# An expert mixer walked in pairs: the large and the small item by turns in parts, instead of one after the other

## The reference

```python
probs = jax.nn.softmax((xt @ router).astype(jnp.float32), axis=-1)
top_p, top_i = lax.top_k(probs, TOP_K)                 # TOP_K = 2 of 8
gates = ...                                            # normalised top_p, 0 elsewhere
for e in range(N_EXPERTS):
    y = y + gates[:, e:e + 1] * swiglu(xt, w_gate_up[e], w_down[e])
```

## Time and profile before

| | us |
|---|---|
| three runs | 1141.86 median, 1139.15 to 1142.47 |
| the profiled execution | 1141.93 |
| its span, first to last instruction | 1140.2 |
| PE busy | 1088.6 (95%) |
| PEld busy | 808.9 (71%) |
| DVE busy | 626.2 (55%) |
| ACT busy | 522.5 (46%) |
| first large unit of the mixer on PE | at 437.89 |
| first large unit of pairs 1, 2, 3 | at 611.00, 783.89, 958.09 |
| last small unit ends on PE | at 1126.66 |

### The profile page before, as it was taken

How to read it: one execution, slowest core, us unless ns; L and a number is a source line. 1 busy time by engine, 2 the same in 40 slices (tenths; PEclk the granted TensorE clock), 3 DMA queues, 4 the chain that set the end, 5 groups by cost and what they waited for, 6 DMA issues and landing times.

```text
span 1140.2 us, 15874 instructions
## 1 busy us (share of the span) xinstructions
PE 1088.6 (95%) x5832; PEld 808.9 (71%) x5832; DVE 626.2 (55%) x710; ACT 522.5 (46%) x576; POOL 23.2 (2%) x94
## 2 busy tenths in 40 slices
PE   9998999999999999999998999998999998999994
PEld 8876888888898787787355787354787445787451
DVE  6865555455654458895106895106897105897102
ACT  6555444344445644775015775014775004676001
POOL 2100000000000000000000000000000000000000
PEclk9999999999999999999999999999999999999998
DMA  9933556555454423998999999999999999999994
GB/s 347 356 112 111 181 182 192 185 185 188 162 176 149 138 77 117 367 362 298 343 417 408 402 418 409 359 416 409 403 418 408 333 413 411 405 414 409 358 412 204
DMA packets 110935, 343.47 MB, mean 301 GB/s; under 512 B 11613, under 2 KB 38282, under 8 KB 100618
## 3 DMA queue, kind: packets, MB, share of 16 engines
q1 hardware_dynamic: 110714, 341.93, 79.6%
q10 hardware_dynamic: 144, 0.52, 0.1%
HBM read 341.37 MB, written 1.05 MB: 300 GB/s over the span
## 4 chain that ended last, share of the span: by engine, by line
PE 78%; DVE 8%; DMA 7%; ACT 3%; issue 2%; SPq 1%; POOL 0%; POOLq 0%; ACTq 0%; DVEq 0%
PE ps L1483 22%; PE ps L1478 18%; PE ps L1480 18%; PE ps L1479 18%; DMA raw<-moe_w_gate_up_dram 5%; DMA raw<-moe_w_down_dram 2%; ACT whi L561 2%; DVE wlo L960 1%; SPq L369 1%; PE ps L1823 1%; DVE wlo L947 1%; DVE wlo L949 1%; DVE h L1212 1%; ACT xs L561 1%; PE ps L1867 1%
## 5 line engine op out<-in xcount | busy, mean ns | idle before, releaser
L561 ACT ACTIVATE whi<-raw 128x2048 fp32r<-128x2048 f32 (+2 forms) x203 | 341.7, 1688 | 247.8 <-PE ps L1480 226.5
L960 DVE TENSOR_TENSOR wlo<-raw,whi 128x2048 fp32r<-128x2048 f32 x151 | 345.4, 2292 | 121.7 <-ACT whi L561 120.6
L1478 PE MATMUL ps<-whi,xhi 128*128 128x512 f32 (+3 forms) x688 | 264.1, 384 | 18.6 <-DVE wlo L960 12.0
L1480 PE MATMUL ps<-wlo,xhi 128*128 128x512 f32 (+3 forms) x688 | 259.4, 377 | 0.0
L1479 PE MATMUL ps<-whi,xlo 128*128 128x512 f32 (+3 forms) x688 | 259.1, 377 | 0.0
L1478 PEld LDWEIGHTS ps<-whi,xhi 128*128 128x128 f32 x688 | 129.5, 188 | 48.3 <-issue 9.2
L1483 PE MATMUL ps<-raw,xs 128*64 128x512 f32 (+2 forms) x1024 | 155.0, 460 | 0.0
L1480 PEld LDWEIGHTS ps<-wlo,xhi 128*128 128x128 f32 x688 | 129.3, 188 | 23.9
L1479 PEld LDWEIGHTS ps<-whi,xlo 128*128 128x128 f32 x688 | 129.5, 188 | 22.1
L1483 PEld LDWEIGHTS ps<-raw,xs 128*64 128x64 f32 x1024 | 68.2, 137 | 81.7 <-issue 71.5
L1478 PE MATMUL ps<-whi,hhi 128*128 128x512 f32 x264 | 105.9, 401 | 0.0
(11 more groups left out here) (298 smaller groups left out, 976.8 us busy)
## 6 DMA issues: line engine op xcount, KB each, us to landing
raw<-moe_w_gate_up_dram SPq DMA_DIRECT2D x256, 512.0 KB, 12.6
raw<-moe_w_down_dram SPq DMA_DIRECT2D x80, 1024.0 KB, 17.0
raw<-moe_w_gate_up_dram SPq DMA_DIRECT2D x96, 384.0 KB, 9.4
raw<-ffn_w_gate_up_dram SPq DMA_DIRECT2D x44, 512.0 KB, 4.9
raw<-ffn_w_down_dram SPq DMA_DIRECT2D x22, 512.0 KB, 4.3
raw<-kv_shared_w_dram SPq DMA_DIRECT2D x16, 512.0 KB, 4.2
raw<-moe_w_gate_up_dram SPq DMA_DIRECT2D x32, 256.0 KB, 9.7
raw<-moe_w_down_dram SPq DMA_DIRECT2D x16, 512.0 KB, 17.9
```

The source lines that it names most:

```text
L561: return nc.scalar.activation(o, i, ACT.Copy, scale=scale)
L960: V.tensor_tensor(wlo[:, s, :].rearrange("p a w -> p (a w)"), raw[:, (hh // 2) % RAW, :], whi[:, s, :].bitcast(F32).rearrange("p a w -> p ...
L1478: pe.matmul(o, a_hi, b_hi, start=start, stop=False, skip_group_check=True)
L1480: return pe.matmul(o, a_hi, b_lo, start=False, stop=stop, skip_group_check=True)
```

## The change

Large and small item of a pair are now worked on by turns: large units 0 to 7, small 0 to 7, large 8 to 15, small 8 to 15, large 16 to 21, small 16 to 21, large 22 to 32, small 22 to 32. Transfers are issued in that order. The large item's groups are transposed after small units 1, 4, 9, 12, 17, 19; the small item's after large units 10, 18, 23, 25. Both gathers for the next pair stand after large unit 27; the large scatter stands after small unit 29, the small scatter after unit 0 of the next pair. Both selections of a pair are transposed in that pair (after large unit 5), ACT copies them out, and POOL's part in `selT` goes away. The rotary products use all 128 rows: `krT` has two copies with the other half zero. Some tensors share memory in another way, and the all-minus-one matrices are made later. What a unit, a gather or a scatter computes stays the same.

```diff
+PARTS = ((0, 8), (8, 16), (16, 22), (22, 33))
+PAIR = [(small, x) for first, end in PARTS for small in (False, True) for x in range(first, end)]
+PLACE = {unit: n for n, unit in enumerate(PAIR)}
...
+            def slot_free(n, p, previous):
+
+                if previous is None and n < RAW:
+                    sp_eng.wait_ge(lo_made, 2 * (U_MOE + n - RAW) + 2)
+                    return
+                small, x = PAIR[n - RAW]
+                of = previous if n < RAW else p
+                if small:
+                    sp_eng.wait_ge(small_used, of * FU + x + 1)
+                else:
+                    sp_eng.wait_ge(lo_made, of * FH + H_MOE + 2 * x + 2)
...
+            pair_loads(0, None, w, None, range(PARTS[0][1]))
+            sp_eng.wait_ge(items_ready, 3)
+            pair_loads(0, None, w, at(1), range(PARTS[0][1], len(PAIR)))
```

On ACT:

```diff
+            def pair(p, split, first=False, last=False):
+
+                for x in range(split, 8):
+                    item_high(x, p)
+                if first:
+                    gathered_small(p)
+                act.wait_ge(sel_tr, p + 1)
+                copy(selT[:, :], ps[:, TR_BANK, 0:SEQ]).then_inc(selT_ready, 1)
+                copy(selTs[:, :], ps[:, TR_BANK, SEQ:2 * SEQ]).then_inc(selT_ready, 1)
+                for part in range(3):
+                    silu(2 * part, p)
+                    silu(2 * part + 1, p)
+                    high(2 * part, p)
+                    high(2 * part + 1, p)
+                    x = 8 * part + (8 if part < 2 else 6)
+                    for n in range(3):
+                        item_high(x + n, p)
+                    small_silu_of(part, p)
+                    item_high(x + 3, p)
+                    hidden(part, p)
+                    if part == 2:
+                        small_silu_of(3, p)
+                    item_high(x + 4, p)
+                    if part == 2:
+                        hidden(3, p)
+                    for n in range(5, 8 if part == 0 else 6):
+                        item_high(x + n, p)
+                if not last:
+                    gathered_high(p + 1)
+                    gathered_small(p + 1)
+                for x in range(28, FU):
+                    item_high(x, p)
```

On DVE:

```diff
+            def pair(p, previous, split, last=False):
+
+                if previous is not None:
+                    add_in(previous, True)
+                for x in range(split, 8):
+                    item_low(x, p)
...
+                if not last:
+                    dve.wait_ge(small_tr, p * SMALL_GROUPS + SMALL_GROUPS)
+                    choose_small()
+                    gathered_low(p + 1)
+                for x in range(28, FU):
+                    item_low(x, p)
...
+                add_in(p, False)
+                dve.wait_ge(small_used, p * FU + FU)
+                V.tensor_copy(ys, ps[:, 4, :]).then_inc(ys_ready, 1)
+                if last:
+                    add_in(p, True)
+                else:
+                    for x in range(3):
+                        item_low(x, p + 1)
```

On PE:

```diff
+            def pair(p, previous, last=False):
+
+                for small, x in PAIR:
+                    if small:
+                        small_unit(x, p)
+                        if x in (1, 4, 9, 12, 17, 19):
+                            transposes((1, 4, 9, 12, 17, 19).index(x), p)
+                        if x == 29:
...
+                            scatter(p)
+                        continue
+                    if x == 1 and previous is not None:
+                        scatter_small(previous)
+                    big_unit(x, p, previous)
+                    if x == 4 and previous is None:
+                        gather_small(p)
...
+                    if x in (10, 18, 23, 25):
+                        small_transposes((10, 18, 23, 25).index(x), p)
+                    if x == 27 and not last:
+                        gather(p + 1)
+                        gather_small(p + 1)
+                if last:
+                    scatter_small(p, last)
...
-                    mm(ps[:, b, a:e], qrT[lo:lo + ROPE, hd // 2, c * P:(c + 1) * P], krT[lo:lo + ROPE, 0:e - a], False, False)
+                    mm(ps[:, b, a:e], qrT[:, hd // 2, c * P:(c + 1) * P], krT[:, hd % 2, 0:e - a], False, False)
```

More of the change, by code:

```diff
@@ L242, in build @@
         x_in = [sem(f"x_in{n}") for n in range(2)]
[L243 removed]
+        h_ready = [None] + [sem(f"h_ready{n}") for n in range(1, 4)]
         consts = sem("consts")
@@ L657, in _ @@
             act.wait_ge(kr_tr, 1)
-            copy(krT[:, :], ps[:, 7, 0:SEQ]).then_inc(krT_ready, 1)
+            for a in range(2):
+                half = slice(a * ROPE, (a + 1) * ROPE)
+                copy(krT[half, a, :], ps[half, 7, 0:SEQ]).then_inc(krT_ready, 1)
             act.wait_ge(qn_done, 3)
@@ new lines, in gathered_small, with silu @@
+            def gathered_small(p):
+                act.wait_ge(gathered_s, p + 1)
+                for k in range(KD):
+                    copy(xs[:, k, :], ps[:, GATHER_SMALL, k * SMALL:(k + 1) * SMALL],
+                         scale=gcol[:, G_FFN1 + k:G_FFN1 + k + 1]).then_inc(xs_ready, 1)
+            def silu(j, p):
+                w = sub_width(j)
+                if j % 2 == 0:
+                    act.wait_ge(even_done, p * 3 + j // 2 + 1)
+                else:
+                    act.wait_ge(used, p * FH + H_MOE + 2 * (8, 16, GU)[j // 2])
+                if j >= 2:
+                    act.wait_ge(gu_tr[2], p * SUB + j - 1)
+                nc.scalar.activation(gm[:, j % 2, 0:w], ps[:, sub_bank(j), 0:w], ACT.Silu).then_inc(silu_done[2], 1)
@@ L982, in x_low @@
                                                op0=ALU.mult, op1=ALU.subtract).then_inc(xlo_ready[n], 1)
+            for a in range(2):
+                V.memset(krT[(1 - a) * ROPE:(2 - a) * ROPE, a, :], 0.0).then_inc(krT_zero, 1)
             dve.wait_ge(g_ready, 1)
@@ new lines, in choose_small, with add_in @@
+            def choose_small():
+                for c in range(TC):
+                    V.tensor_scalar(sels[:, c, :].rearrange("p (a s) -> p a s", a=2),
+                                    iota[:, 0:SMALL].unsqueeze(1).to_broadcast([P, 2, SMALL]), pm[:, 1, 0, c:c + 1], pm[:, 1, 1, c:c + 1],
+                                    ALU.is_equal, ALU.mult).then_inc(sels_ready, 1)
+            def add_in(p, small):
+                dve.wait_ge(gt_ready, p + 1)
+                came, banks, done = (scattered_s, SCATTER_BANK_SMALL, added_s) if small else (scattered, SCATTER_BANK, added)
@@ new lines, in small_transposes @@
+            def small_transposes(j, p):
+                pe.wait_ge(small_gated, p * SMALL_GROUPS + j + 1)
+                if j < 3:
+                    pe.wait_ge(h_lo[2], p * SUB + 2 * j + 2)
+                else:
+                    pe.wait_ge(hT_ready, p * SMALL_GROUPS + 3)
+                for b, block in enumerate(interleaved(gs[:, 0:SMALL_WIDTH[j]], SUB - SMALL_GROUPS + j)):
+                    last = pe.transpose(ps[:, TR_BANK, b * P:(b + 1) * P], block, ident[:, :])
+                last.then_inc(small_tr, 1)
@@ new lines, in scatter, with scatter_small @@
+            def scatter(p):
+                pe.wait_ge(y_lo, p * 2 + 2)
+                for c in range(TC):
+                    for n in range(2):
+                        o = ps[:, SCATTER_BANK[2 * c + n], :].rearrange("p (a s) -> p a s", a=4)
+                        w = selT[:, c * P:(c + 1) * P]
+                        mm(o, w, xhi[:, 4 * n:4 * n + 4, P:SEQ], True, False)
+                        mm(o, w, xlo[:, 4 * n:4 * n + 4, P:SEQ], False, True).then_inc(scattered, 1)
+            def scatter_small(p, last=False):
```

661 lines of the change are left out of this document (260 added, 401 removed).

## The result

| | before | after |
|---|---|---|
| median | 1140.51 us | 1198.80 us |
| the profiled execution | 1141.93 us | 1197.61 us |
| its span | 1140.2 us | 1195.8 us |
| first large unit of the mixer on PE | 437.89 | 433.01 |
| last small unit ends on PE | 1126.66 | 1182.19 |

The ratio is 1.0508 [1.0489, 1.0528]: slower by 5.1%, where 1179 us had been forecast with an upper end of 1192. One execution of after took 1291.2 us at a mean granted clock of 0.834; it is a slow one and is left out.

A forecast was written before the change was run, and what follows sets the result against it. PE's work (166.2 us of pair 1's 172.9) and transfers (168.4) were taken as near one bound. 1141.9 + 32.9 (pairs) - 1.0 (rotary) + 6 (clock) = 1179.8, given as 1179 us, range 1148 to 1192.

The forecast's parts named there:

- Six waits a pair: PE waits at units 12, 20, 22, 27, 28 and the next pair's unit 0, together 16.5 us a pair.
- pair 0's unit 4: PE waits 2.8 us, as that unit's low part stands behind the routing tables and `choose_small` on DVE.
- The work of 166.9 us: PE's work in one mixer pair without waits: 166.2 us before, plus 0.4 for groups and 0.3 for entries.
- The small gather: PE's gather with half the columns, left at 3.5 us because weight loads set it; 1.8 by columns alone.
- the clock's term: Three 6.2 us waits at the gathers let the clock fall, 2.0 us lost each: +6, bounds 0 and 10.
- The waits of 3.1 us stay short of it.: Waits at the pairs' ends were held too short for the clock to fall, which took 3.3 us before.
- forecast without clock: The four mixer pairs from work and waits alone: together 721.7 us against 688.8 before, +32.9.
- the clock's worst: Upper bound of the clock loss at the three gathers, 3.4 us each, 10 in all; +4 in the high end.
- -1.0: Rotary products on 128 rows, ahead of the mixer: eight heads give -0.8 us, with the change of shape -1.0.
- The joints are covered: Rival: ACT and DVE are far enough ahead at units 12, 20, 22 and 27; 1150 us, chance 0.12.
- Faster: Rival: turns even out the load, so PE has no waits but unit 4's; 1117 us, chance 0.09.
- Transfers late: Rival: landings make PE wait 1 us at each of some twenty joints; 1199 us, chance 0.04.

The follow-up runs named there:

- the three reorderings: The after kernel with, separately: splits 28 to 30 ahead of gathered-token copies, 1167.63 us; ACT's joint copies one split later, 1154.40; two next-pair low parts ahead of `ys`, 1180.77.
- The fillers: The after kernel with unread identity matmuls on PE in each of its waits, the order left as it is: 1185.31 us, ratio 1.0396.
- the four executions of one program: Single executions of the after kernel with rotary products on 64 rows again: 1186.61, 1188.73, 1194.45 and 1199.87 us; median 1191.59.
- the version with all orders mended: The after kernel with all three reorderings together, and unit 4's low part ahead of the selections in pair 0: 1122.94 us, ratio 0.9841.
- the version with 29.8 us of waits: The after kernel with ACT's small-item group copies one split later and split 22 ahead of group 5's copy: 1154.40 us, ratio 1.0114.

## Why the prediction was off: its steps against the runs

**The direction and the cause were right.** Six waits a pair were forecast with their places, what ends each and how long; all six are in the trace.

| wait at | forecast | measured in pair 1 |
|---|---|---|
| unit 12, behind `hidden(0)` | 2.1 | 2.14 |
| unit 20, behind `hidden(1)` | 2.1 | 2.09 |
| unit 22, behind `high(5)` | 1.2 | 1.05 |
| unit 27, behind `hidden(3)` | 1.8 | 1.77 |
| unit 28, behind the gathers | 6.2 | 6.03 |
| the next pair's unit 0 | 3.1 | 3.17 |
| pair 0's unit 4 | 2.8 | 1.97 |

That they come from the order is shown by the three reorderings, each of which removed just its own waits. The work of 166.9 us is confirmed by the 167.3 us of a pair without waits. The small gather was left at 3.5 us against the 1.8 of its columns; its 32 records took 3.68 at half the columns.

**The failed step is the clock's term.** It read "+6", with bounds of 0 and 10, and "The waits of 3.1 us stay short of it." They didn't, and neither did several of those of 2.1, 2.0 and 1.8. The error was to take the one fall seen in before, 3.3 us after the last matmul, for the shortest wait that costs anything. An estimate worked out from the stretches in after's trace: a stretch of 3.4 us in matmuls loses half of itself, 1.7. Of a stretch of 6.8 us behind the gathers a part lies in the wait (583.5 to 586.49) and 3.9 us in matmuls, 1.95 lost. By pair:

| pair | forecast without clock | clock: stretches | sum | measured |
|---|---|---|---|---|
| 0 | 187.8 | 2 x 1.7 + 1.95 | 193.2 | 193.9 |
| 1 | 183.4 | 3 x 1.7 + 1.95 | 190.5 | 191.2 |
| 2 | 183.4 | 3 x 1.7 + 1.95 | 190.5 | 191.2 |
| 3 | 167.1 | 3 x 1.7 | 172.2 | 172.9 |

So the clock costs some 24.6 us, not 6. The range failed with the term, since its high end took the clock's worst as +4 over the forecast. The experiments bear the size out. The fillers leave the waits and change the clock: they made the pairs 20.9 us shorter with one stretch left, so some 22.6 in all, and 6.4 in pair 2 where the table reckons 7.05. And the four executions of one program moved with their clock, microsecond for microsecond.

The 0.7 or 0.8 us a pair that the table leaves are small slips of the sum. The prediction counted 0.16 us behind each of before's waits, as a record outlasts its slot, and none behind its own: six a pair, 1.0 us. The six waits of pair 1 measured 16.25 us for its 16.5, and the work 167.3 for 166.9. These come to 1.1 us a pair; with the 6.4 of the filled run that gives 183.4 + 1.1 + 6.4 = 190.9 for pair 2, which took 191.2.

The Trainium skill ("TensorE: Matmul & The Clock Gate", section "HAM oscillation — how this bites in real kernels") has pauses between matmuls put the clock back to low. The trace agrees as to the mechanism and goes further than the prediction drew it, since shorter pauses did it too.

**Ahead of the mixer** -4.9 us instead of -1.0. The transposes come 1.9 us earlier (109.40 to 107.45). The rotary products give 2.2 to 2.3 us where 1.0 was forecast, and the scores begin 0.3 us later. The prediction took the records' lengths, 0.92 against 0.82; by the steps from the group's first matmul to the next instruction it is 0.85 (74.36 to 75.21 in before) against 0.46 (73.84 to 74.30 in after). The other 2.9 us lie in the routing, where before has a low stretch of 6.8 us and after has none. It isn't shown to be the change's: the version with all orders mended has such a stretch there again (from 420.5), and its mixer begins 2.8 us later than after's.

**The rivals.** "The joints are covered" was wrong: sixteen waits, 28.2 us. "Faster" was wrong for this change, but its mechanism exists: with the same walk by turns and ACT's and DVE's orders mended pairs 1 and 2 take 169.5 and 169.0 us, and the time was 1122.9, against the 1117 that it gave. "Transfers late" is wrong for the kernel after; only without the other waits do landings end some, 5.3 us in that version. The threshold named for "faster", 25 us of new waits, is too generous, since waits bring low clock with them: the version with 29.8 us of waits is 14 us slower than before, not 5.

**The three gains don't add.** 31.2 + 44.4 + 18.0 = 93.6 us, all together 75.9. The waits alone add up (18.1 + 28.2 + 9.6 = 55.9 of 58.0). Of the 17.7 us that are missing 5.3 are the waits for landings, which come up only when the others are gone. The remaining 12 or so are put down to the clock: each edit alone also removes or moves stretches that the others remove. That part is an estimate, as what is left.

**Open.** Why one wait of 2.1 us is followed by a low stretch (682.52) and another is not (724.79) was not settled, nor was the kernel before tried with its own waits mended, so what working by turns gives by itself, apart from the orders, isn't known.

## What to carry to other kernels

When work is cut into turns, look at each engine that works through its own program in order, and count what stands ahead of the next thing that the bounding engine will want. A copy that needs the result just made, placed ahead of a split that is wanted one step later, costs the whole chain from that result. Here moving such copies one to three steps later, with no work removed, was worth 76 us of 1199, and turned a loss of 5% into a gain of 1.6%. And when PE is the bound, price a wait at its length and the low clock behind it: here 58 us of waits cost some 23 to 25 us more.

## What the runs showed of the hardware

- The granted clock fell to 0.50 for 3.4 us behind several waits of 1.8 to 3.2 us, and for 6.8 us behind those of 6.0; other waits of 2.1 us in the same execution had no such stretch behind them. One program with the same waits varied between 1186.61 and 1199.87 us by this.
- At the second trip of a run-time loop PE stood still for 2.14 us by itself, and for 1.93 and 4.87 us where short filler matmuls led the body. In the kernel after, where it would wait 3.17 us there anyway, no such idle time shows.
- A gather of 32 records with 64 columns took 3.68 us, one with 128 columns 3.83.
- Four rotary matmuls on 128 rows, half of them zero, took 0.82 us where four on 64 rows took 0.92; to the next instruction it was 0.46 us against 0.85. From the first scores to the transposes behind them, eight heads, this saved 2.2 to 2.3 us (50.6 against 52.9).
